# Building the first expert pair's token rows with one-hot products instead of a gather, in a two-layer decoder trunk

## What is computed

```
def hier_moe(h, w_group, b_group, w_router, b_router, w1, w3, w2):
    # 4 groups of 8 experts; top group, then top 2 experts inside it
    ...
    for g in range(G):
        a = jnp.einsum('nd,edf->nef', t, w1[g])
        b = jnp.einsum('nd,edf->nef', t, w3[g])
        hid = jax.nn.silu(a) * b * combine[:, g, :, None]
        out = out + jnp.einsum('nef,efd->nd', hid, w2[g])
```

## Time and profile before

| | |
|---|---|
| median of three runs | 1146.61 us |
| the profiled execution's own time | 1144.64 us |
| its span, first to last instruction | 1142.9 us |
| TensorE busy | 1039.2 us, 91% |
| VectorE busy | 608.6 us, 53% |
| bytes over the DMA engines | 341.44 MB, mean 299 GB/s |
| chain that ended last | TensorE 76%, DMA 8%, VectorE 5%, the SP queue 4% |
| routing and experts, layer 0 | about 339 to 583 us |
| routing and experts, layer 1 | about 876 to 1129 us |

### The profile page before, as it was taken

The page is one execution under the profiler, slowest core; times in us unless marked ns, Lnnn a source line. Parts: engine busy times, 40 slices in busy tenths (PEclk is TensorE's granted clock), DMA queues, the critical chain, the costliest instruction groups (busy, mean ns, idle before and its releaser), DMA issues.

```text
span 1142.9 us, 15245 instructions
## 1 busy us (share of the span) xinstructions
PE 1039.2 (91%) x5634; PEld 629.0 (55%) x5634; DVE 608.6 (53%) x1464; ACT 327.8 (29%) x894; POOL 91.8 (8%) x129
## 2 busy tenths in 40 slices
PE   4999999999998999898869999899999999979986
PEld 3444444655467666564536565555456766646652
DVE  6899988897646322221246577767235722222224
ACT  4321122874231111111124455666112121111110
POOL 1000000000011111111000000000000111201200
PEclk9999999999998999999999999999999999989999
DMA  9929868918468999999996300300826799999998
GB/s 368 402 76 404 332 255 335 420 57 354 167 267 351 402 417 419 418 418 420 416 404 244 115 1 13 154 19 24 345 89 272 300 418 420 419 411 411 419 416 357
DMA packets 66814, 341.44 MB, mean 299 GB/s; under 512 B 11110, under 2 KB 11366, under 8 KB 36400
## 3 DMA queue, kind: packets, MB, share of 16 engines
q1 hardware_dynamic: 49952, 297.68, 64.4%
q0 software_dynamic: 15120, 37.63, 8.5%
q10 hardware_dynamic: 1664, 5.09, 1.1%
HBM read 320.90 MB, written 37.24 MB: 313 GB/s over the span
## 4 chain that ended last, share of the span: by engine, by line
PE 76%; DMA 8%; DVE 5%; SPq 4%; ACT 3%; issue 3%; DVEq 0%; ACTq 0%; POOLq 0%
PE PP L888 17%; PE PP L681 12%; PE PP L796 10%; PE PP L903 8%; PE PP L703 3%; DMA AHS<-in_moe_w 3%; PE PP L1054 3%; PE PP L1096 3%; PE PP L654 2%; PE PP L1100 2%; PE PP L861 2%; PE PP L740 2%; PE PP L751 2%; PE PP L690 2%; DMA X<-kept_d 2%
## 5 line engine op out<-in xcount | busy, mean ns | idle before, releaser
L681 PE MATMUL PP<-ring,AHS 128*128 128x512 f32 x320 | 139.9, 592 | 0.0
L1963 DVE TENSOR_TENSOR PS<-PS,PP 128x256 f32<-128x256 f32 x33 | 13.9, 421 | 195.5 <-PE PP L888 184.8
L796 PE MATMUL PP<-ring,AHS 128*128 128x512 f32 x256 | 111.3, 593 | 1.4 <-ACT AHS L1425 0.8
L1970 DVE SCALAR_TENSOR_TENSOR PS<-PP,small,GF 128x512 f32<-128x512 f32 x66 | 46.5, 746 | 111.0 <-PE PP L903 100.6
L681 PEld LDWEIGHTS PP<-ring,AHS 128*128 128x128 f32 x320 | 59.7, 190 | 69.8 <-issue 69.8
L888 PE MATMUL PP<-RQK,RV 128*64 128x256 f32 x640 | 73.4, 386 | 9.8 <-issue 7.5
L796 PEld LDWEIGHTS PP<-ring,AHS 128*128 128x128 f32 x256 | 48.1, 190 | 59.7 <-issue 59.7
L888 PE MATMUL PP<-ring,RV 128*64 128x256 f32 (+1 forms) x608 | 76.6, 392 | 4.5 <-ACT RV L1459 1.7
L1483 ACT ACTIVATE PS<-PP 128x256 f32<-128x256 f32 x33 | 12.6, 383 | 216.2 <-PE PP L888 174.2
L888 PE MATMUL PP<-AHS,RV 128*64 128x256 f32 x640 | 71.9, 380 | 2.3 <-issue 2.3
L888 PEld LDWEIGHTS PP<-RQK,RV 128*64 128x64 f32 x640 | 55.1, 139 | 30.9 <-issue 18.1
(11 more groups left out here) (346 smaller groups left out, 1665.8 us busy)
## 6 DMA issues: line engine op xcount, KB each, us to landing
AHS<-in_moe_w SPq DMA_DIRECT2D x61, 1024.0 KB
ring<-in_moe_w SPq DMA_DIRECT2D x58, 1024.0 KB, 23.9
RQK<-in_moe_w SPq DMA_DIRECT2D x52, 1024.0 KB, 16.7
ring<-in_ada_t SPq DMA_DIRECT2D x22, 1024.0 KB
AHS<-in_ada_t SPq DMA_DIRECT2D x18, 1024.0 KB
X<-in_moe_w SPq DMA_DIRECT2D x16, 1024.0 KB, 23.0
ring<-in_da_w_qkv SPq DMA_DIRECT2D x10, 1024.0 KB, 9.8
RQK<-in_ada_t SPq DMA_DIRECT2D x8, 1024.0 KB, 6.8
```

Of the source, the lines that this page charges most:

```text
L681: last = mm(PB[qkv_bank(n)][:, :], HT[:, c, t * P:(t + 1) * P], us[c // 4][:, (c % 4) * NH:(c % 4 + 1) * NH], start=c == 0, stop=c == C - 1)
L796: last = mm(PB[2 * t + n][:, :], (OT, OTM)[l][:, k, t * P:(t + 1) * P], us[k // 2][:, (k % 2) * D + n * NH:(k % 2) * D + (n + 1) * NH], st ...
L1970: last = stt(ysb[b][:, cols], PB[5 + m][:, :], weight, GF[:, cols], ALU.mult, ALU.mult)
```

## The change

Pair 0 gets its rows without a gather. VectorE makes for each of the four token tiles a 128 x 128 one-hot matrix `first_hot` (token by place), in float32, in the first 512 columns of X, from the place minus 4096 for every choice that is not in pair 0. TensorE multiplies the normalised rows in SBUF (XN) by it, 4 tiles by 8 chunks of 128 columns, and gets pair 0's rows already transposed. The 22 dummy products are gone. VectorE must wait for kept_out before it writes into X, and does so ahead of its wait for rank. The scaled rows of pair 0 go to GM. The list idx is made only after pair 0 was scaled. SP loads unit 19 without a wait for gathers, then waits for the rows' product and loads unit 18. `weigh` is split: the weights stay ahead of step 0, the tables' factors go to step 0 behind the scaling of pair 1, with tables_out after them; `weigh_places` moves on TensorE from step 0 to step 1, behind its first product.

```diff
@@ SP
-                for b in range(2):
-                    sp.wait_ge(sem(f"gath{b}"), 16 * (PAIRS // 2 * l + 1))
-                for u in (18, 19):
-                    expert_unit(l, u)
+                expert_unit(l, 19)
+                sp.wait_ge(sem("xgt"), PAIRS * l + 1)
+                expert_unit(l, 18)
@@ TensorE
+            def first_rows(l):
+                wait(pe, sem("xA"), PAIRS * l)
+                wait(pe, sem("xD"), PAIRS * l)
+                for t in range(T):
+                    pe.wait_ge(sem("hotp"), 6 * l + t + 1)
+                    for c in range(C):
+                        last = mm(PB[4 * (c // 4) + c % 2][:, (c // 2 % 2) * P:(c // 2 % 2 + 1) * P],
+                                  XN[:, t, c * P:(c + 1) * P], first_hot[:, t, :],
+                                  start=t == 0 and c // 2 % 2 == 0, stop=t == T - 1 and c // 2 % 2 == 1)
+                        if t == T - 1 and c == C // 2 - 1:
+                            last.then_inc(sem("xh"), 1)
+                last.then_inc(sem("xgt"), 1)
                 keep_busy(3, 5)
+                first_rows(l)
...
-                pe.wait_ge(sem("idx"), 2 * l + 1)
-                keep_busy(3, 22)
@@ TensorE, expert_step
                 into_hidden(PB[2], b, w, 0, tiles, range(0 if n else C // 2, C)).then_inc(sem("a"), 1)
+                if n == 1:
+                    weigh_places(l)
...
+                if n == 0:
+                    pe.wait_ge(sem("idx"), 2 * l + 1)
                 wait(pe, sem("hid"), m)
                 into_hidden(PB[3], b, w, 1, tiles, range(C // 2 if n == LAST else 0, C)).then_inc(sem("b"), 1)
-                if n == 0:
-                    weigh_places(l)
@@ VectorE, gate
+                link(ts(first_half, hot_step[:, :, 0], -1.0, 4096.0, ALU.add, ALU.mult))
+                link(tt(first_half, first_half, half_of, ALU.add))
+                dve.wait_ge(sem("kept_out"), 16 * T * (l + 1))
                 dve.wait_ge(sem("rank"), 2 * l + 1)
...
+                tt(first_place, raw, first_half, ALU.add)
...
+                link(tt(first_place, first_place, over_cap, ALU.add))
+                first_places(0, 0)
+                link(first_places(1, 0))
+                first_places(0, 1)
+                first_places(2, 0)
+                first_places(1, 1)
+                link(first_places(3, 0))
+                first_places(2, 1)
+                first_places(3, 1)
...
+                modulate_first_pair(l)
+                dve.wait_ge(sem("tab"), 2 * l + 1)
+                ts(second[:, 0:PAIRS], PB[3][:, 0:PAIRS], S + 0.5, -float(S), ALU.is_le, ALU.mult)
@@ VectorE, expert_step
                 hidden(sem("hid"))
-                if n == 0:
-                    tables_out(l)
                 if n < LAST:
                     modulate_pair(l, n + 1)
...
+                if n == 0:
+                    weigh(l)
+                    tables_out(l)
                 dve.wait_ge(sem("y"), m + 1)
@@ GpSimd
-                for n in range(2):
-                    gather_pair(n)
+                gather_pair(1)
```

More of the change, by code:

```diff
@@ L145, in wait, with gathered @@
     eng.wait_ge(sem, value)
+def gathered(l, n):
+    return PAIRS // 2 * l + n // 2 if n % 2 else (PAIRS // 2 - 1) * l + n // 2 - 1
 def ada_steps(n):
@@ L351, in build @@
         xgT = [view(RV, 2048 + 1024 * b, C, P) for b in range(2)]
+        first_xgT = view(GM, 0, C, P)
+        first_hot = X[:, 0, 0:T * P].rearrange("p (t q) -> p t q", t=T)
         ysb = [view(PS, 1024 * b, D) for b in range(2)]
@@ L374, in build @@
         half_of, place, over_cap, raw = scratch(PS, 2 * T), scratch(PS, 2 * T), scratch(PS, 2 * T), scratch(PS, 2 * T)
+        first_half, first_place = scratch(PS, 2 * T), scratch(PS, 2 * T)
         assert at[0] <= 2816
@@ L842, in route @@
                 keep_busy(3, 5)
+                first_rows(l)
                 for h in range(2):
-                    pe.wait_ge(sem("hotp"), 2 * l + h + 1)
+                    pe.wait_ge(sem("hotp"), 6 * l + T + h + 1)
                     for j in range(T * h, T * h + T):
-                        last = mm(PB[2][:, 0:PAIRS], hot_place[:, j], hot_token[:, j], start=j == 0, stop=j == 2 * T - 1)
+                        last = mm(PB[3][:, 0:PAIRS], hot_place[:, j], hot_token[:, j], start=j == 0, stop=j == 2 * T - 1)
                 last.then_inc(sem("tab"), 1)
-                pe.wait_ge(sem("idx"), 2 * l + 1)
-                keep_busy(3, 22)
             def weigh_places(l):
@@ L870, in turn_pair @@
                 turn_rows(xg[b], sem("xgt"))
[L872 to L882, removed]
             def into_hidden(o, b, w, m, tiles, chunks=range(C)):
@@ L924, in expert_step @@
                 tiles = ((0, CAP, 0), (CAP, 2 * CAP, 1))
-                b, m, w = n % 2, PAIRS * l + n, stored(l, n)
+                b, m, w = xgT[n % 2] if n else first_xgT, PAIRS * l + n, stored(l, n)
                 def arrived(k):
@@ L1871, in gate @@
                 link(red(extra, cmp, AX.X, ALU.add))
+                modulate_first_pair(l)
+                dve.wait_ge(sem("tab"), 2 * l + 1)
+                ts(second[:, 0:PAIRS], PB[3][:, 0:PAIRS], S + 0.5, -float(S), ALU.is_le, ALU.mult)
+                link(ts(empty[:, 0:PAIRS], PB[3][:, 0:PAIRS], -1.0, 2.0 * S, ALU.mult, ALU.add))
+                tt(idx[:, 0:PAIRS], empty[:, 0:PAIRS], second[:, 0:PAIRS], ALU.add).then_inc(sem("idx"), 1)
                 cur = extra
@@ L1886, in gate, with weights @@
                 link(red(slotf, slots, AX.X, ALU.add))
-            def weigh(l):
+            def weights(l):
                 slots = picked.rearrange("p t k e -> p (t k) e")
@@ L2016, in experts @@
                 dve.wait_ge(sem("gf"), 16 * (l + 1))
-                modulate_first_pair(l)
-                weigh(l)
+                weights(l)
                 for n in range(BETWEEN):
@@ L2317, in gather_pair @@
                     if n < PAIRS:
-                        b, q = n % 2, PAIRS // 2 * l + n // 2
-                        wait(pool, sem("xgt"), PAIRS * l + n - 1 if n >= 2 else 0)
-                        wait(pool, sem(f"gath{b}"), 16 * q)
+                        b = n % 2
+                        pool.wait_ge(sem("xgt"), PAIRS * l + max(1, n - 1))
+                        wait(pool, sem(f"gath{b}"), 16 * gathered(l, n))
                         gather(xg[b], idx[:, n:n + 1], sem(f"gath{b}"))
```

26 lines of the change are left out of this document (14 added, 12 removed).

## The result

| | before | after |
|---|---|---|
| median of 20 runs each | 1145.12 us (1140.86 to 1148.72) | 1147.74 us (1145.38 to 1151.71) |
| ratio | | 1.003, 95% interval 1.0018 to 1.0041 |
| the profiled execution's own time | 1144.64 us | 1151.71 us |
| its span and granted clock | 1142.9 us, 0.987 | 1150.0 us, 0.981 |

The account below looks back on a forecast made before the run. Weight stream bounds layer 0, TensorE's chain to the overflow tile layer 1. Layer 1 +4.4 + 2.6, layer 0 -2.9 + 0.8, together +4.9 on 1144.64 us, plus 2.0 for the median: 1151.5 us, range 1142 to 1158.

Parts of the forecast that it names:

- Which resource bounds which layer: Expert stages: the weight stream sets layer 0's end, TensorE's chain from pair 0 to the overflow tile sets layer 1's.
- The rival in which DMA sets both layers: Both layers' ends follow the weight stream, about -3 to -5 us together, 1142.5 us; chance 0.15.
- The wait for the saves: Routing: VectorE's new wait for kept_out ahead of the ranks costs 1.4 us in layer 1, 0.8 us in layer 0.
- The one-hot product: Routing: TensorE starts 2.4 us after the wait, product takes 7.5 us; layer 1's pair 0 product starts 1.3 us later.
- The fall that had one chance in two: Granted clock falls to half before layer 1's product in one of two cases, counted as +0.9 us.
- Step 0 in layer 1: Ends where it ended before, about 907.8 us: shift 0, bounds -0.6 and +3.5.
- The late-gather rival: Pair 1's gather lands 9 us after issue, TensorE waits 4 us in layer 1's step 0: 1155.5 us; chance 0.13.
- Step 1 in layer 1: Step grows 4.4 us: weigh_places 1.8, and 2.6 of TensorE waiting for `hidden` behind tables and control.
- The clock's sum: Granted clock's falls after new idle times cost +2.6 us in layer 1 and +0.8 us in layer 0.
- Layer 0: Pair 0's product releases SP's issue of unit 20 sooner, so the weight stream gains 2.9 us.
- The sum: Both layers together +4.9 us on the profiled 1144.64 us: 1149.5, put at 1151.5 for the median.
- The range's low end: Low end of the forecast's own case: +0.5 us, with no fall of the clock and the gather early.

Follow-up runs that it names:

- e5: Kernel before with 24 dummy products added in step 3 of layer 1 only; 1147.89 against 1144.2 us, ratio 1.0037.
- e6: Kernel before with 24 dummy products added in step 3 of layer 0 only; 1143.92 against 1144.2 us, ratio 0.9987.
- e9: e8 with pair 3's gather issued ahead of pair 0's scatter; 1141.38 against 1145.02 us, ratio 0.9967.
- e8: Changed kernel with control block behind pair 2's scaling, one-hot tiles in GM without the save wait, unit 18 not waiting for the product; 1142.88 us, ratio 0.9986.
- e7: Kernel before with only the moves of weights, tables and weigh_places into step 1, no one-hot product; 1146.61 against 1144.2 us, ratio 1.0018.
- e12: e9 with the control block back ahead of `hidden` in step 1; 1145.14 against 1144.39 us, ratio 1.0005.
- e1: Changed kernel measured again, nothing altered; 1147.74 against 1144.23 us for the kernel before, ratio 1.003.
- e2: Changed kernel with the control block moved behind the scaling of pair 2; 1148.47 against 1144.23 us, ratio 1.0032.
- e11: e9 measured again, nothing altered; 1139.75 against 1144.39 us for the kernel before, ratio 0.995.
- e4: Changed kernel with dummy products added in TensorE's idle times, nine before the one-hot product and eight in step 1; 1150.22 against 1144.23 us, ratio 1.0036.
- e3: Changed kernel with the one-hot tiles in a free part of GM, so nothing waits for the saves; 1146.11 against 1144.23 us, ratio 1.0019.

## Why the prediction was right, point by point

**Which resource bounds which layer**: held. The gap of the DMA engines widened, SP's issue moved by 7.3 us with the tile's output, and e5 and e6 show the split: 5.5 us of TensorE cost 3.7 us in layer 1 and nothing in layer 0. The rival in which DMA sets both layers is refuted. But the prediction passed over how near the two are in layer 1: before's gap of 3 us at a share of 0.79 is 0.6 us of transfers, and layer 1 of e9, with its tile 1.7 us sooner, ends no sooner.

**The wait for the saves**: 1.4 and 0.8 us predicted, 1.39 and 0.73 us in the trace.

**The one-hot product**: TensorE starts 2.55 us after VectorE's first operation behind the wait (887.02 - 884.47; predicted 2.4), and its 64 instructions take 7.41 us at full clock (predicted 7.5): 0.116 us each. The figure of the Trainium skill, "TensorE: Matmul & The Clock Gate", section on the back-to-back issue gap, would have made it 5.2 us, an estimate; three profiles at full clock give 7.38 to 7.41 us, so for 128 columns in float32 the row was the right base. Pair 0's product starts 20.24 us after R1 (896.24 - 876.0) instead of 17.1 us (893.51 - 876.4): +3.1 us, where the steps had +1.3 without a fall of the clock and +3.0 with one. The fall that had one chance in two took place; it did in all three profiles with the wait, and in two of four with the old routing, so only part of it is the change's.

**Step 0 in layer 1**: it ended 1.5 us later from R1 (32.83 for 31.37 us). That is the predicted 0 and the 1.7 us of the fall that the first product had been charged with. The late-gather rival is refuted for pair 1: the gather landed 3.9 us after its issue, 4.4 in layer 0, and nothing waited. The Trainium skill, "DMA: Bandwidth & Descriptors", section on the anatomy of a SWDGE DMA, gave an estimate of 3.2 us and the same conclusion; the landings are 0.7 to 1.2 us above it. The rival had the wrong pair: it was pair 3's gather that came late, once the steps before it were shorter (e8).

**Step 1 in layer 1**: the step grew by 7.47 us. weigh_places is 2.0 of it (1.8 predicted), the stall 2.17 (2.6 predicted), and the clock 2.98 (L911 takes 6.63 us under half clock for 3.65 at full). Here a term was mis-sized: each fall had been put at 1.7 us, after the 3.4 us stretch in the earlier trace rows; this one lasted 6.7 us. In e7 a shorter one cost 1.7 us (5.35 for 3.65), so both lengths occur.

**The clock's sum**: predicted as +2.6 in layer 1 and +0.8 in layer 0. In the profile of after it was 1.6 + 3.0 in layer 1, and 0 in layer 0's step 1, where the clock didn't fall (in e12 it did, at 382.6 us). Against that, before has a fall of 6.8 us near the tile, at 1011 us, where after's lasts 3.4 us. That is why the +8.9 us at y1 are +7.7 at the tile: from y8 to the tile it is 17.2 us in the profiles without a fall there (e1, e2, e9, e11), 18.7 to 18.9 with one of 3.4 us (18.8 in after), and 20.0 to 20.3 with one of 6.8 us (before, e4, e7). The prediction counted only the falls that the change makes, and not those it may move or take away.

**Layer 0**: SP's issue came 3.2 us sooner by the clock of the span, 2.9 predicted. At pair 15's output 2.8 us of it are left in this profile, 0.5 in e1's and -0.1 in e2's, while e7, which has no new product, shows a gain of 2.3, and e5, unchanged in layer 0, one of 1.3. e1 and e2 have the early R0. The earlier start is certain; how much of it reaches the end of layer 0 isn't settled.

**The sum**: 7.7 at the tile against 7.0 predicted for layer 1, and -2.8 against -2.1 for layer 0, so +4.9 on both sides, which is more agreement than the terms earn: the larger fall in step 1 was offset by the smaller one at the tile. The medians say +2.6 (+3.5 beside e1). The likeliest place for the difference to 4.9 is the clock's term: a profiled execution shows a fall or none, while over the executions the kernel before has some of the same falls, as e6 and e7 show for the one before pair 0's product. How often each comes in the untraced executions no run shows. e3 bears on this, where the wait and its fall are 3.0 us at y0, nothing at the tile and 1.6 us in the median; e11 and e12 show the other case, a fall that is paid nearly in full. The 2.0 us that were added for the median of the first three runs of before (1146.61) were too much as well: over 20 runs it is 1145.12. Of the 3.8 us by which the forecast lies above the measured median, 2.3 are the former difference (4.9 to 2.6) and 1.5 this addition. The range's low end was not quite its terms either: 4.4 less 0.6 and 2.9 is +0.9 and not +0.5.

## What to carry to other kernels

Before you price a stall, find for each stage whether the engine's chain or the transfer stream ends last; the same 5.5 us cost 3.7 us in one layer and nothing in the other. When work is moved to a later step, follow what now stands ahead of the next step's first operation on the engine's queue: here a bookkeeping block of 4.0 us, harmless beside products, came to stand ahead of `hidden` and, in the kernels with the tiles in GM, cost 3 to 5 us until it was moved one step on. The gain shrinks where the other side takes over: once the gap of the transfers is nearly closed, a tile that is 1.7 or 2.2 us sooner moves the end by nothing (e9) or by 1.5 us (e11). And a new way of doing one part should not borrow a buffer that a transfer still reads, when another one is free.

## What the runs showed of the hardware

In these traces the granted clock's falls, from 1.00 to 0.50, last 3.4 or about 6.7 us, and in one profile 10.2 us. A stall of 2.17 us in step 1 was followed by half clock in after's layer 1, in e1, e3, e7 and e12, and not in after's layer 0. Dummy products in the stalls were followed by no fall there, and the median was still 1150.2 against 1147.7 us (e4). From pair 15's output to R1 it takes about 295 or about 298 us; the six profiles with 298, of before's code and of the changed one, have a fall near 724 us and a longer one near 600 us. A comparison of two single profiles can be off by that much, and counting each layer from its own start takes it out.
